# A hybrid decoder block on one core: order of the input stage's first units, S5 tables in stacked form, two units of a quarter interleaved, S5 loads in two parts

## What is computed

```python
h = rmsnorm(x, norm_attn)
proj = h @ w_in                      # 1024 x 2048: q | k | v | u, 512 columns each
# S5 branch: 32 groups of 16 channels, each driving a 64-dim complex diagonal state
dt = exp(log_dt); lam_bar = exp(lam * dt)
b_bar = ((lam_bar - 1) / lam) * b_c
bu = einsum('gnc,bsgc->bsgn', b_bar, u)
_, states = associative_scan(combine, (a, bu), axis=1)      # over positions
y = einsum('gcn,bsgn->bsgc', c_c, states).real + d_skip * u
y = gelu(y); y = y * sigmoid(y @ w_glu + b_glu); y = rmsnorm(y, ssm_gain)
```

## Time and profile before

| | |
|---|---|
| median of 3 runs | 2393.55 us (2392.29 to 2399.78) |
| the profiled execution | 2386.33 us, span 2384.7 us |
| PE busy | 2074.4 us, 87% of the span |
| VectorE busy | 1410.3 us, 59% |
| mean granted clock of TensorE | 0.936 |
| input stage: first unit, last unit's end | 37.25 us, 473.5 us |
| S5: start, first states | 481.8 us, 496.9 us |

### The profile page before, as it was taken

One profiled execution on the slowest core, in us unless ns is written; L12 is line 12 of the kernel. 1 busy time (PEld: TensorE's weight loads), 2 busy tenths in 40 slices (PEclk: granted clock), 3 DMA queues, 4 the chain that ended last, 5 costly groups with the idle time before them and its releaser, 6 DMA issues. The chain is left out here.

```text
span 2384.7 us, 32604 instructions
## 1 busy us (share of the span) xinstructions
PE 2074.4 (87%) x10318; PEld 1702.6 (71%) x10319; DVE 1410.3 (59%) x2646; ACT 1073.1 (45%) x1581; POOL 516.3 (22%) x631
## 2 busy tenths in 40 slices
PE   4989799858868898986999759999999999999980
PEld 3877677658447786876888637888888888888860
DVE  2789745445228686775534477567558857354544
ACT  3322211122317777776222226566547846354443
POOL 2001000024000000000000014545454645344430
PEclk9999899979969999998999859999999999999995
DMA  7565765462137314301433449779769979666737
GB/s 217 166 229 199 261 220 198 162 220 92 52 91 168 89 36 115 71 1 53 145 129 133 154 142 369 251 257 338 277 223 345 396 276 337 197 233 204 264 79 299
DMA packets 169819, 458.40 MB, mean 192 GB/s; under 512 B 20400, under 2 KB 69632, under 8 KB 143872
## 3 DMA queue, kind: packets, MB, share of 16 engines
q1 hardware_dynamic: 122608, 284.90, 34.7%
q0 software_dynamic: 30848, 138.24, 18.8%
q10 hardware_dynamic: 16272, 34.09, 4.1%
HBM read 342.08 MB, written 115.10 MB: 192 GB/s over the span
## 5 line engine op out<-in xcount | busy, mean ns | idle before, releaser
L1861 DVE TENSOR_TENSOR w_down_lo<-w_down_raw,w_down_hi 128x2048 fp32r<-128x2048 f32 x64 | 144.2, 2288 | 125.5 <-ACT w_down_hi L1798 125.4
L1093 DVE CUSTOM_DVE_ANT_0 scores<-c_bank,alibi 128x512 f32<-128x512 f32 (+3 forms) x320 | 176.3, 607 | 39.0 <-PE c_bank L1206 39.0
L1232 PE MATMUL c_bank<-v_head,map_T 128*128 128x128 f32 x1088 | 150.7, 284 | 31.9 <-ACT map_T L1148 30.5
L1945 PE MATMUL m_bank<-w_down_hi,hidden_T_hi 128*128 128x512 f32 x392 | 160.0, 408 | 6.8 <-DVE w_down_lo L1861 6.8
L1232 PEld LDWEIGHTS c_bank<-v_head,map_T 128*128 128x128 f32 x1088 | 133.8, 194 | 44.5 <-ACT map_T L1148 43.9
L1861 DVE TENSOR_TENSOR w_gate_lo<-w_gate_raw,w_gate_hi 128x2048 fp32r<-128x2048 f32 x63 | 141.6, 2288 | 33.5 <-ACT w_gate_hi L1798 32.5
L1139 ACT ACTIVATE scores<-scores,neg_max 128x128 f32<-128x128 f32 (+15 forms) x128 | 153.4, 1199 | 17.6 <-DVE neg_max L1097 17.5
L1924 PE MATMUL m_bank<-w_gate_hi,rows_T_hi 128*128 128x512 f32 x392 | 156.0, 398 | 4.0 <-issue 2.6
L1924 PE MATMUL m_bank<-w_up_hi,rows_T_hi 128*128 128x512 f32 x392 | 159.0, 406 | 0.0
L1946 PE MATMUL m_bank<-w_down_lo,hidden_T_hi 128*128 128x512 f32 x392 | 156.3, 399 | 0.0
L1925 PE MATMUL m_bank<-w_gate_lo,rows_T_hi 128*128 128x512 f32 x392 | 155.8, 397 | 0.0
(11 more groups left out here) (411 smaller groups left out, 5181.9 us busy)
## 6 DMA issues: line engine op xcount, KB each, us to landing
w_gate_raw<-in_w_gate_dram SPq DMA_DIRECT2D x64, 1024.0 KB
w_up_raw<-in_w_up_dram SPq DMA_DIRECT2D x64, 1024.0 KB, 8.2
w_down_raw<-in_w_down_dram POOLq DMA_DIRECT2D x64, 1024.0 KB
hT_d<-hT_parts SPq DMA_DIRECT2D x32, 512.0 KB, 5.9
hT_parts<-hT_d SPq DMA_DIRECT2D x32, 512.0 KB, 9.0
u_tok<-in_x_dram SPq DMA_DIRECT2D x16, 512.0 KB
qT_d<-proj_out ACTq DMA_DIRECT2D x32, 256.0 KB, 3.2
kT_d<-proj_out ACTq DMA_DIRECT2D x32, 256.0 KB, 3.2
```

The source lines that it names most:

```text
L1093: dve.tensor_tensor_reduce(S[:, s, m, c * BANK:c * BANK + w], bank[2 * (n % 2) + m][:, 0:w], ramp[:, x0:x0 + w], SLOPES[h], -BIG, ALU.add, ...
L1232: last = pe.matmul(bank[6 + u % 2][:, 0:VD], aT[:, n % 2, b * P:(b + 1) * P], v[:, h % 2, kt], start=kt == 0, stop=kt == u % NT)
L1861: dve.tensor_tensor(wlo[w][:, halves[i]], raw[w][:, halves[i]], whi[w][:, halves[i]], ALU.subtract).then_inc(lo_done[w], 1)
L1945: pe.matmul(DN[h][:], hh[:, k], whi[2][:, part(k)], start=k == 0, stop=False)
```

## The change

- **Start.** Order of units (0 is V of tile 0, then V of tile 1, U of tile 0, U of tile 1, from then on as before); transposes of tile 1 between units 0 and 1; unit 0 waits for each half of the weights only at its k-step; splits, copies and norms in the order that this needs; gain on SP's queue behind x0, x2 behind U; POOL waits for x1 before its first load; the Sqrt table is loaded ahead.
- **Tables.** Real and imaginary parts lie behind each other in one tile (`pw`, `tab`, `anc`, `sm`), and a rotation (`turn`) is two operations on both parts and two on one. Levels 0 to 2 are made once for all 32 groups (`first_tab`, eight columns). Anchors take seven operations.
- **Pieces.** `prepare` is cut smaller: tiles 1 to 14, then one piece for each unit from 34 to 57. Two batches stand at tiles (PE: 10 and 12), six at units 36, 40, 44, 48, 52, 56. The taps are written behind unit 59.
- **Columns.** Units 6 and 7 of a quarter run interleaved, k-step by k-step.
- **S5.** Loads of batch 0 in two parts of four groups: W and tables, then taps, then Q, then the rest.

```diff
+    T0 = 8
+    order = [(0, 0), (1, 0), (0, 1), (1, 1)] + [(i, slot) for i in range(2, NT) for slot in range(2)]
...
+        WITH_TILE = 2
+        w_at_tile = [9, 11]
+        w_at_unit = lambda b: P1 + 2 + 4 * (b - WITH_TILE)
+        batch_at_tile = {i + 1: b for b, i in enumerate(w_at_tile)}
+        batch_at_unit = {w_at_unit(b) + 2: b for b in range(WITH_TILE, NHB)}
...
                 x_load(0)
+                sp.dma_start(gain, a["norm_attn"].to_broadcast([P, D])).then_inc(gain_in, 16)
                 w_raw(V, 0)
                 w_raw(V, 1)
                 x_load(1)
-                x_load(2)
                 for half in range(2):
                     sp.wait_ge(wlo_done, 1 + half)
                     w_raw(UU, half)
+                x_load(2)
...
             @block.gpsimd
             def _(pool):
+                pool.wait_ge(x_in[1], 16)
                 pool.dma_start(sm[:, 0, :], a["ssm_log_dt"].to_broadcast([P, NG])).then_inc(small_in, 16)
...
             def _(act):
-                act.dma_start(gain, a["norm_attn"].to_broadcast([P, D])).then_inc(gain_in, 16)
+                act.preload_act_table(ACT.Sqrt)
...
                 square(0)
                 root(0)
                 w_hi(0, 0, 1)
+                rows_hi(0)
+                w_hi(0, 1, 1)
                 square(1)
                 root(1)
-                w_hi(0, 1, 1)
-                rows_hi(0)
-                for half in range(2):
-                    w_hi(1, half, 2)
                 for i in range(NT):
                     if i + 1 < NT:
                         rows_hi(i + 1)
+                    if i == 0:
+                        for half in range(2):
+                            w_hi(1, half, 2)
...
+                def turn(src, out, cos, sin, t):
+
+                    step(dve.tensor_tensor(out, src, cos, ALU.mult))
+                    step(dve.tensor_tensor(t, src, sin, ALU.mult))
+                    step(dve.tensor_tensor(out[:, 0], out[:, 0], t[:, 1], ALU.subtract))
+                    step(dve.tensor_tensor(out[:, 1], out[:, 1], t[:, 0], ALU.add))
...
+                def level(table, e, gs, n):
+                    k = 1 << e
+                    by = [anc[:, e, r, gs].rearrange("p (o g q) -> p o g q", o=1, q=1).to_broadcast([P, 2, n, k]) for r in range(2)]
+                    t = tmp[:, 0:2 * n * k].rearrange("p (r g k) -> p r g k", r=2, g=n)
+                    turn(table[:, :, :, 0:k], table[:, :, :, k:2 * k], by[0], by[1], t)
...
+                    elif i == 8:
+                        anchors(range(8, 10))
+                        first_levels()
+                    elif i == 9:
+                        matrices_w(0)
+                        matrices_q(0)
+                    elif i == 10:
+                        levels(0, range(3, 7))
+                    elif i == 11:
+                        levels_end(0)
+                        matrices_w(1)
+                    elif i == 12:
+                        matrices_q(1)
+                    elif i == 13:
+                        levels(1, range(3, 7))
+                    elif i == 14:
+                        levels_end(1)
+
+                def prepare_at_unit(n):
+                    b, part = WITH_TILE + (n - w_at_unit(WITH_TILE)) // 4, (n - w_at_unit(WITH_TILE)) % 4
...
+                    if part == 0:
+                        matrices_w(b)
+                    elif part == 1:
+                        matrices_q(b)
+                    elif part == 2:
+                        levels(b, range(3, 7))
                     else:
-                        levels((n - 5) // 2, range(4, 8))
+                        levels_end(b)
...
+                def columns(ns):
+                    t, j = (ns[0] - P1) // 8, (ns[0] - P1) % 8
+                    slot = j // 4
+                    pe.wait_ge(ev_done, ns[-1] - 2)
+                    if ns[-1] >= P1 + 3:
+                        pe.wait_ge(lo_done, ns[-1] - P1 - 2)
                     for k in range(KT):
...
+                        if j == 6 and k < KT - 1:
                             last.then_inc(slice_used, 1)
...
                 for n in range(P1, UNITS):
+                    j = (n - P1) % 8
                     if n in batch_at_unit:
                         batch(batch_at_unit[n])
-                    columns(n)
+                    if j < 6:
+                        columns((n,))
+                    elif j == 6:
+                        columns((n, n + 1))
...
+                first, later = slice(0, 4), slice(4, GB)
+                load_w(0, first, w_first)
+                load_t(0, first, t_first)
+                sp.wait_ge(m_zero, 1)
+                for i in range(CH):
+                    sp.dma_start(M[i * GC:(i + 1) * GC, i:, :], d["taps"][0:CH - i].rearrange("t q g c -> q t (g c)")
+                                 ).then_inc(m_in, 16)
+                load_q(0, first, q_first)
                 for b in range(NB):
                     if b >= 2:
                         sp.wait_ge(y_done, 4 * (b - 1))
...
+                    gs = slice(0, GB) if b else later
+                    load_w(b, gs, batch_in[b % 2])
+                    load_t(b, gs, batch_in[b % 2])
+                    load_q(b, gs, batch_in[b % 2])
```

More of the change, by code:

```diff
@@ new lines, in first_levels @@
+                def first_levels():
+                    step(dve.memset(first_tab[:, 0, :, 0:1], 1.0))
+                    step(dve.memset(first_tab[:, 1, :, 0:1], 0.0))
+                    for e in range(3):
+                        level(first_tab, e, slice(0, NG), NG)
+                up = lambda t: t.rearrange("p g (k o) -> p g k o", o=1).to_broadcast([P, HB, CH, GC])
+                across = lambda t: t.rearrange("p g (o c) -> p g o c", o=1).to_broadcast([P, HB, CH, GC])
+                groups = lambda b: slice(b * HB, (b + 1) * HB)
@@ L537, in matrices, with matrices_w @@
+                def matrices_w(b):
+                    gs = groups(b)
                     if b:
@@ L570, in prepare, with levels_end, prepare_at_tile @@
-                def prepare(n):
-                    if n == 0:
+                            step(dve.tensor_copy(tab[:, :, :, 0:T0], first_tab[:, :, groups(b)]))
+                        level(tab, e, groups(b), HB)
+                def levels_end(b):
+                    levels(b, (7,))
+                    dve.tensor_copy(tmp[:, 0:1], tab[:, 0, 0, 0:1]).then_inc(tables, 1)
+                    dve.wait_ge(tables, b + 1)
+                def prepare_at_tile(i):
+                    if i == 1:
+                        steps_of_time()
+                    elif i == 2:
@@ L660, in rows @@
                     for k in range(KT):
+                        if i == 0 and k % 4 == 0:
+                            pe.wait_ge(whi_done, 2 * slot + 1 + k // 4)
+                            pe.wait_ge(wlo_done, 2 * slot + 1 + k // 4)
                         pe.matmul(o, tile_hi(i, k), whi[:, slot, k], start=k == 0, stop=False)
```

224 lines of the change are left out of this document (106 added, 118 removed).

## The result

The changed kernel takes **2338.18 us**, the median of 4 runs (2335.25 to 2342.22); beside it the kernel before takes 2396.28 (2392.29 to 2399.78, also 4 runs). The ratio is 0.9767, with a 95% interval of 0.9748 to 0.9785. The forecast was 2341, the range 2323 to 2359. The profiled execution is the fastest of the four, 2335.25 us with a span of 2333.7 and a mean granted clock of 0.945; that of before had 2386.33, 2384.7 and 0.936. Between these two spans lie 51.0 us, and the sum of the prediction had 52.3.

A forecast was written before the change was run, and what follows sets the result against it. PE was taken as bound by its own work plus gaps between units, which also cost clock. Terms -16.5 -16.6 -12.9 +0.2 +1.0 -7.5 = -52.3 us gave 2334.0 against the profiled 2386.33, 2341 against the median; range 2323 to 2359.

The forecast's parts named there:

- Start: Until unit 2 begins: reordered loads, splits and units let it begin at 36.9 instead of 53.35 us, -16.5 us.
- rival (b): Start stays bound by its loads, DMA falling to 190 GB/s: 8 us less gain, 2349 us; chance 0.17.
- Tiles: Units 2 to 31: smaller VectorE slices fit, one new wait at batch 1; 202.3 to 185.7 us, -16.6 us.
- First Q unit: Before the first Q unit: no slice stands at tile 15, so the gap from 255.68 to 268.56 goes, -12.9 us.
- Columns: Units 32 to 63: waits for hT slices go, new waits for batches' W matrices at quarter ends; +0.2 us.
- rival (c): ScalarE's chain of stores is late at all quarter ends, unit 6's copy 3 to 4 us late: +11, 2352; chance 0.12.
- Stage's end: After PE's last unit: units 62 and 63 end together, so 9.3 us instead of 8.3, +1.0 us.
- S5: S5's start to VectorE's pair 2: loads in two parts bring it to 24.0 us from 31.7, -7.5 us.
- (a): Waits of 2.5 to 2.9 us leave the clock up, cold units and batches fall away: 16 us, 2325; chance 0.14.
- (d): Stacked VectorE operations with three free dimensions and a broadcast cost more than their elements say: 2407 us; chance 0.02.
- (e): The change doesn't do what it says; only the 12.9 us and a few more come: 2375 us; chance 0.03.
- Later stages: Stages behind S5 are not touched; no term in the sum.

The follow-up runs named there:

- experiment 2: Changed kernel, but POOL does not wait for x1 before its 14 small loads: 2338.66 us (2 runs).
- experiment 3: Changed kernel, but VectorE's preparation in slices as large as before (eight anchors at tile 6, batch 1's levels together at tile 15): 2341.36 us.
- experiment 4: Changed kernel with its new operations, but the preparation and batches stand where they stood before the change, four batches in the tiles: 2323.54 us.
- Experiment 5: Changed kernel, but each turn of levels and powers takes six operations on separate real and imaginary parts instead of four stacked: 2338.77 us.
- experiment 8: Two single edits of the changed kernel: batch 0 of S5 loaded whole, 2348.88 us; or S5's taps loads held until the first tables landed, 2335.97 us.
- experiment 9: No new kernel: compares profiles of the untouched gate stage, 103.8 to 117.9 us with the same instructions, in step with granted clock 0.91 to 0.80.

## Why the prediction was right, point by point

The number came, and most of the mechanism, with these exceptions.

- **Start**, -16.5, measured -12.8. Unit 0's terms were too small: V0 landed at 12.81 instead of 11 (unit 0 at 18.35, not 16.5), and unit 0 took 8.36 us instead of 6.85. The steps behind it, 2.7 us to unit 1 and 5.5 to unit 2, came as worked out. That the loads would be free of the small ones was right, and experiment 2 puts 4.6 us on it; rival (b) did not come.
- **Tiles**, -16.6, measured -18.2. Batch 1's wait was 2.18 for 2.5, and with its batch and unit it cost 6.9 for the 7.0 of the sum; 1.3 of the 1.6 us are unit 2, which was not as cold as assumed (6.00 us). The reason held only in part. I had put it on the slice over 8.3 us; experiments 3 and 4 show the sum over many tiles, and that the cheaper operations alone suffice. Experiment 5 shows that the tiles don't need the stacking either, once two batches have moved.
- **First Q unit**, -12.9, measured -12.5. The reason given, "No slice stands at tile 15 now", is one of two that do: before, the slice of tile 15 ran from 254.16 to 265.98 us, 11.8 of the wait's 12.7, because VectorE came to it late. With the lighter work a slice there costs 5.1 us (experiment 4) or nothing (experiment 3).
- **Columns**, +0.2, measured +2.0, with errors that cancel. The slices' waits went, and the three quarter ends waited 2.85 us each as forecast; with batch and unit they cost 18.2 us for the forecast 21.9. The joint wait before unit 38 came (2.5 us for 2.7) but did not take the clock. What was missed: batches 4 and 6 in mid-quarter, 10.2 us with their gaps and units where 2.7 were in the sum. The sum took these batches as warm, without a wait, but ScalarE's copy of unit 39 waited 10.5 us for a store and held up VectorE's chain up to batch 4. That is the mechanism of rival (c), in another place than the one I gave it.
- **Stage's end**, +1.0, measured +1.6: 10.15 us where 9.3 were worked out.
- **S5**, -7.5 (31.7 less the prediction's own 24.0 is 7.7), measured -5.2 at pair 2 and -6.8 up to the gate (-7.5 against experiment 8's whole loads). The step that failed is "W and tables 6 us after the start". Undisturbed they need 7.7 (experiment 8), and with the taps issued beside them at 4.4 they had 11.8. The taps then follow at the pace that I had given them (135 GB/s for 137), so that the first outputs were at 19.3, or 18.9 with the taps held, and not at 16.8. The prediction's estimate from the Trainium skill ("DMA: Bandwidth & Descriptors", whose rules for kernel authors want at least 1 MiB per DMA and whose table has 138 GB/s for 64 KB) had 2.7 us less gain, 4.8, and that is nearer to 5.2 than my 7.5; but small pieces aren't all of the reason, as 3.8 us of the delay came from the taps. The rate of these first 1.5 MB alone, 203 GB/s over their 7.7 us, lies between the page's 138 and my 392, and the whole loads of experiment 8 lose 7.5 us all the same.
- **Rivals.** (a) came in one place, unit 38; the waits of 2.85 us at the quarter ends all took the clock (units of 7.05, 7.21 and 6.93 us). (d) is excluded by the 1.22 us of the stacked operations, (e) by the table of stages.
- **Later stages** "not touched" was right for the code and wrong for the clock: 4.2 us of the 51.0 come from behind S5 with the granted clock, as in experiment 9. So some of the agreement of 2334.0 with 2335.25 is luck: without them the forecast of 52.3 stands against 46.8.

## What to carry to other kernels

Ask of an engine that prepares beside the critical one how much it has to do over a stretch of many tiles, not only how long one piece is: a piece of 13.4 us followed by an empty tile cost 1.4 us, a load of 89% over 100 us made everything late. When a change makes a gap vanish, look at what each wait behind it now depends on; here six waits of under 3 us, 14.6 in all, went but for 2.0 when the consumer was placed one unit later, and the stages became 22.5 us shorter, because the clock had nearly doubled their price. Interleaving two units frees their buffers early and moves their results together to the end, so it should stand only where the first is wanted and the second does no harm.

## What the runs showed of the hardware

A gap of about 2.8 us before unit 38 stands in eight of the profiles, in seven with the same PE instructions around it, in the eighth with a batch one unit nearer. (The gap is counted from the start of unit 37, less a unit at full speed.) In three the unit ran at full clock (gaps of 2.70, 2.90 and 2.78 us; 5.56, 5.56 and 5.54 us for the unit), in five it did not (2.78, 2.78, 2.89, 2.77 and 2.68; 7.14, 7.15, 7.14, 7.14 and 7.08 us). The length of the gap does not decide; what does is not shown. So each such wait had a price of 0 or some 1.6 us beside its own length, and a forecast with ten of them is uncertain by several microseconds for that alone, as an estimate.
